# Two of eight token tiles of a retrieval layer computed over all experts on TensorE, six gathered, and the work ahead of the gathers compressed from 128 slots to 62

## The reference

```
q = (h @ w_q).reshape(bsz, s, PEER_HEADS, 2, PEER_HALF)         # 8 heads
scores = einsum('bshpd,pkd->bshpk', q, sub_keys)                # 2 x 128 keys
s_top, i_top = top_k(scores, 16)
cand = (s_top[..., 0, :, None] + s_top[..., 1, None, :]).reshape(..., 256)
best, c_idx = top_k(cand, 16)                                   # 8 x 16 = 128 picks a token
expert = i1 * 128 + i2 ;  gates = softmax(best)
act = einsum('bthkd,btd->bthk', u[expert], x)
w = gates * gelu(act)
out = einsum('bthk,bthkd->btd', w, v[expert])                   # then h <- LN(alpha*h + out)
```

## Time and profile before

| | |
|---|---|
| median of 3 runs | 4433.24 us |
| the profiled execution | 4419.49 us, its span 4417.6 us |
| DVE busy / PE busy / POOL busy | 53% / 55% / 54% of the span |
| gathers | 2048 of 512 KB, 1073.87 MB |

### The profile page before, as it was taken

The page is one execution under the profiler, slowest core; times in us unless marked ns, Lnnn a source line. Parts: engine busy times, 40 slices in busy tenths (PEclk is TensorE's granted clock), DMA queues, the critical chain, the costliest instruction groups (busy, mean ns, idle before and its releaser), DMA issues.

```text
span 4417.6 us, 33711 instructions
## 1 busy us (share of the span) xinstructions
PE 2446.3 (55%) x10844; PEld 1289.7 (29%) x10844; DVE 2342.8 (53%) x4908; ACT 891.9 (20%) x2805; POOL 2404.9 (54%) x2104
## 2 busy tenths in 40 slices
PE   8999878988881543532543453354345335423333
PEld 5778756565640121210120121012012001200000
DVE  3330077674008557557546655755665675575443
ACT  1310033232021211211211221121122112111111
POOL 1333100000006777777777767777777777777775
PEclk9999989999895766755765675576578557655555
DMA  2322242120507998999989999999999999999998
GB/s 84 128 95 86 85 149 69 43 72 29 201 34 260 351 340 326 362 363 352 359 330 363 352 351 363 350 362 359 365 347 359 363 356 367 345 358 358 373 359 307
DMA packets 348199, 1201.38 MB, mean 272 GB/s; under 512 B 37248, under 2 KB 60544, under 8 KB 346384
## 3 DMA queue, kind: packets, MB, share of 16 engines
q0 software_dynamic: 294912, 1073.87, 65.6%
q1 hardware_dynamic: 53136, 125.68, 7.9%
HBM read 1166.90 MB, written 32.51 MB: 272 GB/s over the span
## 4 chain that ended last, share of the span: by engine, by line
POOL 43%; issue 13%; PE 6%; DMA 5%; DVE 2%; another core or an unknown queue 2%; ACT 0%; POOLq 0%; DVEq 0%; ACTq 0%
POOL v_ring L1295 22%; POOL u_ring L1283 21%; DMA v_ring<-in_v_dram,idx_v 4%; PE acc L1327 3%; PE small L1381 2%; DVE u_ring L1523 0%; DMA u_ring<-in_u_dram,idx 0%; PE wide L1366 0%; PE wide L1352 0%; PE wide L1391 0%; DVE work L1723 0%; DVE ihalf L1726 0%; DVE work L1718 0%; DVE idx_v L1618 0%
## 5 line engine op out<-in xcount | busy, mean ns | idle before, releaser
L1523 DVE CUSTOM_DVE_ANT_0 u_ring<-u_ring,h 128x1024 f32<-128x1024 f32 x1024 | 1250.5, 1224 | 1170.2 <-DMA u_ring<-in_u_dram,idx 1089.6
L1327 PE MATMUL acc<-v_ring,spread_w 128*32 128x512 f32 x4096 | 873.4, 988 | 1762.6 <-DMA v_ring<-in_v_dram,idx_v 1644.3
L1283 POOL DMA_INDIRECT u_ring<-in_u_dram,idx x1024 | 1091.1, 1066 | 1120.7 <-DVE idx L1728 803.5
L1295 POOL DMA_INDIRECT v_ring<-in_v_dram,idx_v x1024 | 1163.9, 1137 | 472.3 <-issue 286.8
L1327 PEld LDWEIGHTS acc<-v_ring,spread_w 128*32 128x32 f32 x4096 | 168.3, 152 | 2378.5 <-issue 2188.4
L1439 ACT ACTIVATE spread_w<-comb,w_v 128x32 f32<-128x32 f32 x1024 | 248.0, 310 | 1097.4 <-PE acc L1327 452.8
L1423 ACT ACTIVATE gelu_v<-act_u 32x4 f32<-32x4 f32 x1024 | 212.7, 208 | 980.9 <-DVE act_u L1523 689.9
L680 PE MATMUL mix_bank<-w_out,mixT 128*128 128x512 f32 x512 | 227.1, 600 | 2.4 <-ACT mixT L870 2.4
L1381 PE MATMUL small<-work,pwq 128*128 128x128 f32 x1024 | 144.6, 298 | 32.0 <-issue 30.4
L1381 PEld LDWEIGHTS small<-work,pwq 128*128 128x128 f32 x1024 | 134.1, 210 | 68.0 <-issue 66.2
L264 PE MATMUL group<-w_nat_high,x_high 128*128 128x512 f32 x384 | 150.1, 391 | 3.7 <-ACT padded L383 3.7
(11 more groups left out here) (254 smaller groups left out, 3291.1 us busy)
## 6 DMA issues: line engine op xcount, KB each, us to landing
u_ring<-in_u_dram,idx POOLq DMA_INDIRECT x1024
v_ring<-in_v_dram,idx_v POOLq DMA_INDIRECT x1024
w_nat<-in_w_nat_dram SPq DMA_DIRECT2D x6, 2048.0 KB, 8.7
nat_dram<-stage SPq DMA_DIRECT2D x48, 256.0 KB, 2.2
scanT_dram<-stage SPq DMA_DIRECT2D x22, 512.0 KB, 2.9
w_tr<-in_w_tr_dram SPq DMA_DIRECT2D x18, 512.0 KB, 4.0
gate_in<-nat_dram SPq DMA_DIRECT2D x16, 512.0 KB, 4.3
qkb<-scanT_dram SPq DMA_DIRECT2D x24, 256.0 KB, 5.2
```

The costliest lines, as they stand in the source:

```text
L1283: pool.indirect_dma_start(out=u_ring[:, g % U_RING, :], out_offset=None, in_=peer_u, in_offset=bass.IndirectOffsetOnAxis(ap=idx[:, s, n:n ...
L1295: pool.indirect_dma_start(out=v_ring[:, g % V_RING, :], out_offset=None, in_=peer_v, in_offset=bass.IndirectOffsetOnAxis(ap=idx_v[:, s, n: ...
L1327: last = pe.matmul(acc[c * QUAD:(c + 1) * QUAD, half * 512:(half + 1) * 512], spread_w[:, slot, :], v_ring[:, slot, half * 512:(half + 1) ...
L1523: dve.tensor_tensor_reduce(out=row, in0=row, in1=h2[:, s, :], scale=1.0, scalar=0.0, op0=ALU.mult, op1=ALU.add, accum_out=act_u[:, (n // T ...
```

## The change

- **Six gathered tiles, two dense.** Tiles 0 to 5 go through 768 slots as before. Tiles 6 and 7 (256 tokens together) gather nothing. Their `act` is computed for all 16384 experts: for each first key i, `dense_u(i)` multiplies 128 rows of u (transposed on the host as `uT`, 512 KB) with the 256 tokens, 8 matmuls of 256 columns; ACT takes the gelu; DVE (`dense_weigh`) multiplies by the tokens' gates for these 128 experts; `dense_v(i)` multiplies with 128 rows of v, 4 matmuls of 512 columns, and accumulates in `wide` over all 128 i.
- **The gate matrix** `chosen` (128 second keys x 64 first keys x 256 tokens, in the place of the memory tables) comes from one-hot products, in two halves of 64 first keys: for 8 tokens at a time (64 turns in all) DVE compares and multiplies (`hots`, 512 + 1024 + 512 columns), PE does 8 matmuls of 64 columns (`choose`), ACT copies (`keep_chosen`).
- **Ticks.** A half is 16 ticks of two such turns and 128 ticks that alternate `dense_u` and `dense_v`. The 288 ticks lie in the 277 slots 475 to 751, in each slot behind its gather, dot or combine. SP streams `uT` and v through two rings of 3 buffers in the place of `pwq`.
- **Fronts run ahead.** Fronts 1 to 7 follow one another from slot 39 on, 62 slots each: 58 stages in 27 slots, 40 chunks in 35. `idx`, `idx_v` and `gates_v` keep 5 tiles. `h2` of tiles 1 to 7 goes through DRAM (`store_h2`, `load_h2`).
- `norm3` of the two dense tiles comes at slots 754 to 761.

```diff
-CHUNKS_AT = 58
+FRONT_STAGES = 58
+STAGE_SLOTS = 27
+CHUNK_SLOTS = 35
+GATHERED = 6
+DENSE = TILES - GATHERED
+DT = DENSE * P
+KEPT = 5
+HALF_KEYS = NKEYS // 2
+TOKENS = 8
+GROUPS = DT // TOKENS
+GROUP_TICKS = GROUPS // 2
+HALF_TICKS = GROUP_TICKS + 2 * HALF_KEYS
+STREAM = 3
...
+        SPAN = STAGE_SLOTS + CHUNK_SLOTS
+        DENSE_AT = FIRST_LATE + (TILES - 1) * SPAN + 2
+        DENSE_END = SLOTS - 16
...
+                def load_uT(i):
+                    if i == 0:
+                        sp.wait_ge(pq_made, TILES)
+                    if i >= STREAM:
+                        sp.wait_ge(uT_used, i - STREAM + 1)
+                    sp.dma_start(uT_ring[:, i % STREAM, :, :], peer_uT[i]).then_inc(uT_landed[i % STREAM], 16)
...
+                def choose(b, q):
+                    turn = b * GROUPS + q
+                    pe.wait_ge(hot_ready, turn + 1)
+                    if turn < 2:
+                        pe.wait_ge(dense_ready, 1)
+                    elif q < 2:
+                        pe.wait_ge(gelu_d_done, HALF_KEYS)
+                    else:
+                        pe.wait_ge(chosen_ready, turn - 1)
+                    for j in range(TOKENS):
+                        at = q % 2 * 512 + j * HALF_KEYS
+                        last = pe.matmul(small[:, at:at + HALF_KEYS], hot2[:, q % 2, j, :], hot1[:, q % 2, j, :],
+                                         start=True, stop=True)
+                    last.then_inc(chosen_made, 1)
...
+                def dense_u(i):
+                    pe.wait_ge(uT_landed[i % STREAM], 16 * (i // STREAM + 1))
...
+                    for k in range(KC):
+                        last = pe.matmul(small[:, at:at + DT], uT_ring[:, i % STREAM, k, :], dense_hT[:, k, :],
+                                         start=(k == 0), stop=(k == KC - 1))
+                    last.then_inc(uT_used, 1)
...
+                def dense_v(i):
+                    pe.wait_ge(vb_landed[i % STREAM], 16 * (i // STREAM + 1))
+                    pe.wait_ge(wT_ready, i + 1)
...
+                            last = pe.matmul(wide[:, at:at + 512], chosen[:, i % HALF_KEYS, e * P:(e + 1) * P],
+                                             vb_ring[:, i % STREAM, c * 512:(c + 1) * 512],
+                                             start=(i == 0), stop=(i == NKEYS - 1))
...
+                def dense_gelu(i):
+                    act.wait_ge(uT_used, i + 1)
...
+                def hots(b, q):
+                    turn = b * GROUPS + q
...
+                    if turn >= 2:
+                        dve.wait_ge(chosen_made, turn - 1)
...
+                    dve.tensor_tensor(hot1[:, q % 2, :, :], names(b * HALF_KEYS, HALF_KEYS), per_token(0, HALF_KEYS),
+                                      ALU.is_equal).then_inc(hot_step, 1)
+                    dve.tensor_tensor(hot2[:, q % 2, :, :], names(0, NKEYS), per_token(1, NKEYS), ALU.is_equal)
+                    dve.wait_ge(hot_step, turn + 1)
+                    dve.tensor_tensor(hot1[:, q % 2, :, :], hot1[:, q % 2, :, :], per_token(2, HALF_KEYS),
+                                      ALU.mult).then_inc(hot_ready, 1)
...
+                def dense_weigh(i):
+                    dve.wait_ge(gelu_d_done, i + 1)
...
+                    dve.tensor_tensor(at, at, gelu_d[:, i % 2, :], ALU.mult).then_inc(wT_ready, 1)
```

More of the change, by code:

```diff
@@ new lines, in dense @@
+                def dense(tick):
+                    b, r = tick // HALF_TICKS, tick % HALF_TICKS
+                    if r < GROUP_TICKS:
+                        for q in (2 * r, 2 * r + 1):
+                            choose(b, q)
+                    at, base = r - GROUP_TICKS, b * HALF_KEYS
+                    if at in (0, 1):
+                        dense_u(base + at)
+                    elif at in (2 * HALF_KEYS - 2, 2 * HALF_KEYS - 1):
+                        dense_v(base + at - HALF_KEYS)
+                    elif at >= 2 and at % 2 == 0:
+                        dense_u(base + at // 2 + 1)
+                    elif at >= 3:
+                        dense_v(base + (at - 3) // 2)
@@ L1404, in body @@
                             combine(*lagged(t, s, n))
-                        if next_front:
-                            front(t + 1, 1 - s, n - late(t))
+                        slot = PICKS * t + n
+                        f, stages = stages_at(slot)
+                        for stage in stages:
+                            front(f, f % 2, stage)
+                        if slot == DENSE_AT:
+                            turn_dense()
+                        for tick in ticks_at(slot):
+                            dense(tick)
                 def last(t, s):
@@ L1475, in front @@
                         last.then_inc(keyscores_ready, 1)
-                    if f > 0 and n + late(f - 1) == chunk_slot(f, 33):
-                        gate_exps(range(PHEADS), f + 2)
                 def gate_exps(hs, turn):
@@ L1504, in body @@
                             gate_exps(range(FIRST_HEADS, PHEADS), 2)
-                        if next_front:
-                            front(t + 1, 1 - s, n - late(t))
+                        slot = PICKS * t + n
+                        f, stages = stages_at(slot)
+                        for stage in stages:
+                            front(f, f % 2, stage)
+                        f, chunks = chunks_at(slot)
+                        if 33 in chunks:
+                            gate_exps(range(PHEADS), f + 2)
+                        if slot == DENSE_AT:
+                            turned_dense()
+                        for tick in ticks_at(slot):
+                            dense(tick)
+                        for e in range(DENSE):
+                            if slot == DENSE_END + 3 + 5 * e:
+                                norm3(GATHERED + e)
                 def last(t, s):
@@ new lines, in dense_weigh, with dense @@
+                def dense_weigh(i):
+                    dve.wait_ge(gelu_d_done, i + 1)
+                    dve.wait_ge(chosen_ready, GROUPS * (i // HALF_KEYS + 1))
+                    at = chosen[:, i % HALF_KEYS, :]
+                    dve.tensor_tensor(at, at, gelu_d[:, i % 2, :], ALU.mult).then_inc(wT_ready, 1)
+                def dense(tick):
+                    b, r = tick // HALF_TICKS, tick % HALF_TICKS
+                    if r < GROUP_TICKS:
+                        for q in (2 * r, 2 * r + 1):
+                            hots(b, q)
+                    at, base = r - GROUP_TICKS, b * HALF_KEYS
+                    if at in (2, 3):
+                        dense_weigh(base + at - 2)
+                    elif at >= 4 and at % 2 == 0 and at <= 2 * HALF_KEYS - 2:
+                        dense_weigh(base + at // 2)
@@ L1746, in _ @@
                     dve.tensor_copy(comb[rows, :], ident[rows, rows]).then_inc(comb_ready, 1)
-                for n in range(CHUNKS_AT):
+                for n in range(FRONT_STAGES):
                     front(0, 0, n)
```

331 lines of the change are left out of this document (250 added, 81 removed).

## The result

| | before | after |
|---|---|---|
| time, median of 4 runs | 4432.7 us (4403.4 to 4433.8) | 4200.7 us (4197.9 to 4208.6) |
| profiled execution: time, span | 4419.5, 4417.6 us | 4208.6, 4206.7 us |
| ratio to before, 95% interval | | 0.9495 [0.9454, 0.9536] |

The account below looks back on a forecast made before the run. Slots were taken as bound by bytes (2.95 us each, 355 GB/s), packed chunks by DVE and its links. Span: 2826 + 10 + 192 + 1152 + 47 + 5 + 48 = 4280 us, 4296 as median, said 4300; range 4150 to 4520.

Parts of the forecast that it names:

- The balance of bytes and chains: Whole kernel: by bytes 377 us gained (755 saved, 378 for streams), of which fronts lose 103 and the gate matrix 101.
- turning: Between fronts and gate matrix: transposes and copies of h2 and the picks, 10 us, or 0 if rings cover it.
- the signs named ahead: Fronts: dots 3.1 to 3.25 us, DMA below 0.92; gate matrix: DVE over 90%; dense: 1150 us, PE clock over 0.9.
- the first rival: Bytes rule nearly everywhere: fronts end at 2740 us, gate matrix 5.6 and dense 4.35 us a tick, 4165 us; chance 0.16.
- The dense tick, 4.5 us: Dense products, 256 ticks in 246 slots: bytes and PE nearly equal limits, 4.5 us a tick, 1152 us.
- the limit by bytes: Dense products: 1.53 MB a tick takes 4.32 us, also given as the lower bound.
- order, hand-offs and SP's waits: Dense products: allowance, with two limits at nearly the same height, that brings the tick to 4.5 us; 46 us lost (256 x 0.18).
- The gate matrix, 192 us: 32 ticks in about 31 slots: DVE decides at 6.0 us a tick, PE 4.7 at the upper clock, 8.9 at the lower.
- The fronts, 1383 us: Fronts 1 to 7, slots 39 to 472: serial chain, 194 us each (stages 99, chunks 95), plus 5 ahead and 20 for norms.
- 14 us for combines and 8 for gaps: Stages of a front: additions to 72.7 us unhindered, for combines and for "issue" gaps in PE's query product.
- PE at the lower clock in the dense part: Rival: PE's clock drops in waits; 4684 us at clock 0.75, 5183 all at the lower level; chance 0.18.
- The fronts' longer chain of 218 us: Rival: 218 us a front through PE's issue gaps and waits between engines; 4468 us, with luck 4400; chance 0.11.

Follow-up runs that it names:

- before_again: The kernel before, unchanged, profiled again in a later session: 4384.5 us.
- no_dense: The changed kernel without the streams of u and v, the gate matrix and the dense products: 3590.6 us.
- half_choose: The changed kernel with 4 of 8 one-hot products of a turn left out from the third turn on: 4092.4 us.
- bf16_hots: The changed kernel with the one-hot matrices in bfloat16, rounding the gates of the dense tiles: 4149.2 us, ratio 0.9457 to the kernel before.
- half_query: The changed kernel with each front's query product over 4 of 8 pieces of the width: 4090.0 us.
- stage33: The changed kernel with a front's 62 slots divided 33 for stages and 29 for chunks, instead of 27 and 35: 4207.9 us, ratio 0.9583 to the kernel before.
- after_again: The changed kernel without an edit, run again in a later session: 4187.1 us, ratio 0.9544 to the kernel before.
- half_products: The changed kernel with half of PE's dense products left out, all DMAs and waits kept: 4077.6 us.
- half_stream: The changed kernel with only 64 of 128 partitions of each streamed block loaded after the first three: 4121.4 us.

## Why the prediction was right, and where it was off

**The balance of bytes and chains: right.** The 256 slots did go, and the gain was eaten in part by the fronts and the gate matrix, as said. Fronts slow the slots (1431.5/433 = 3.31 us instead of 2.95), and the dense products run at PE's upper clock.

**The number: in part luck.** Fronts, turning and gate matrix took 95 us more than forecast, the dense products and the rest of the slots 168 less. Only because these have opposite signs does the time lie within 2.4% of the forecast; the gain was 232 us and not 133. The session mattered too: the prediction was built on a trace with slow gathers and measured with slow gathers. Of the signs named ahead, the DMA share in the fronts held (0.91), and so did PE's full row at a clock over 0.9 in the dense part. But the slots of the fronts took 3.31 us and not 3.1 to 3.25, DVE was 84% busy in the gate matrix and not over 90%, and the dense products took 1002 us and not 1150. Two slips in its sums change nothing: the first rival's terms give 4163 us, not 4165, and PE's tick in the gate matrix with a quarter of a combine at 1.92 us is 4.5, not 4.7.

**The dense tick, 4.5 us: the term that was mis-sized, -150 us.** PE's records had the prices of the earlier trace rows, and 4.0 us was on record as PE's floor. Above it I put the limit by bytes at 4.32 us, PE at 4.1 to 4.3 for a clock of 0.92 to 0.97, and 0.18 us on top of 4.32 for "order, hand-offs and SP's waits". All three were too high. The limit by bytes is the larger part, (4.32 - 3.91) x 256 = 105 us. It was taken from 355 GB/s, the rate of POOL's gathers beside fronts; with a third of the bytes on SP's queue and no fronts the same engines moved 385 and 388 GB/s, which makes 1.53/0.388 = 3.94 us, so my own lower bound of 4.32 lay above what was measured. before_again has 2.84 us a slot where no front runs, 369 GB/s, and no_dense 403 in another session, so 355 was no limit of the engines; how the difference divides between fronts, queues and session isn't shown. The allowance of 0.18 us is the other 46 us: PE never waited, 0.0 and 2.2 us in the groups above. I put that down to the rings of stream blocks and gathered rows, whose depth no run changed. And the clock was 0.99 and 1.00.

**The gate matrix, 192 us: +40 us.** Counts were right, the limit was wrong. The prediction held DVE (6.0) against PE at the upper clock (4.7) and put PE at the lower clock (8.9) in the bounds. The granted clock was 0.59 and 0.68, although PE was 94 to 96% busy, and PE then took 232.3/32 = 7.3 us a tick. half_choose and bf16_hots both show it: take work from PE and the stretch shrinks until DVE is full. The stretches of the earlier trace rows in which a busy PE had a high clock are other work. The one at 1.00 has mostly products of 256 and 512 columns. The one at 0.93 has products of 64 to 512, those of 512 being the largest group (112.5 us of 266), with PEld busy 181 us of 266. In the gate matrix all have 64, and PEld is busy 97.41 us of PE's 107.74 in the first stretch; that it is this which keeps the clock down was not tried apart.

**The fronts, 1383 us: +48 us.** Ten of them come before the first cycle: its copy in stage 2 started 15.3 us behind the dot of slot 39, where the sum had 5. The trace of before has 14.6 us there; what holds the copy wasn't tried. The stages took 94 to 101 us in after, as forecast (99), but half_query and stage33 show that landings at combines and dots hold them in part; my 14 us for combines and 8 for gaps stood in for that. The chunks took 99 to 102 us without a norm and 105 with one, where the sum had 95 and 101.6. I had taken the idle 10.7 us of the earlier chunk stretch as room for the added dots, but with four more of them DVE is still idle for 9.9 us of 99.9 (after_again above), so most of it was links in the chain. Between a cycle's picks and the next copy went 1.7 to 4.1 us that the sum didn't have. So the cycles were 2 to 9 us too long, 38 us over seven.

**The rivals.** PE at the lower clock in the dense part didn't happen: 0.99 and 1.00. The rule of the Trainium skill (TensorE: Matmul & The Clock Gate, HAM oscillation) speaks of products shorter than the wait for the next block; here PE had no such wait, as the line against it had said, so the trace doesn't contradict the rule, it lacks its condition. That bytes rule nearly everywhere was wrong for the fronts (0.91 of the DMA share, 329 GB/s) and nearly true of the dense part (half_products gives back only 4 to 5%). The fronts' longer chain of 218 us was not reached.

## What to carry to other kernels

Where PE's row is going to be full, price it by its records at their clock and add nothing for hand-offs, if rings stand between it and its suppliers; look instead for the resource whose "limit" was read under other users. A busy PE isn't yet a fast one: read the granted clock by the kind of product, and set both levels against the other engine before naming the limit. And a gain against a kernel that gathers is to be measured beside that kernel, on the same chip and at the same time.

## What the runs showed of the hardware

**The rate of gathers changes between chips and moments.** The kernel before took 4433, 4386, 4182 and 4189 us in four sessions; the 4386 and the 4189 were the same chip some ten minutes apart, each the median of 11 runs within 1%. Gathers alone took 2.84 us a slot in one (before_again, slots 900 to 1020) and 2.61 in the other (no_dense, slots 491 to 750), the mean packet of POOL's queue 0.158 and 0.147 us (its share times 16 engines times the length, over its count, from 3000 to 3300 and from 2800 to 3560 us). What causes it no run here shows. It matters for the ratio: the dense part is PE's and takes the same in both, 1280.7 us from slot 475 to slot 767 in after and 1277.6 in half_query, while the kernel before gathers in all its 1024 slots. So the change is worth 5% where gathers are slow, and at the faster rate less: half_query, which even leaves work out, was at 4090.0 against 4189.1, 2.4%, and half_stream, on another chip and with part of the stream left out, at 4121.4 against 4182.2, 1.5%.

**The share of busy DMA engines isn't a measure of room.** It read 0.96 at 358 GB/s, 1.03 at 325 (half_stream), 1.00 at 388 and 1.03 at 409 (half_products).
